# Norm factors moved behind the products, raw rows of x transposed beside the last sum, three chunks in the first feed-forward

## What is computed

```python
def rms_norm(x, g):
    y = x * rsqrt(mean(x * x, axis=-1) + EPS)
    return y * g
# first block, for each of 2 layers
h = rms_norm(x, attn_norm[l]); proj = h @ w_in[l]       # q k v, u, latent (c_q, c_kv, k_rope)
x = x + mixed @ w_out[l]
h = rms_norm(x, ffn_norm[l])
x = x + (silu(h @ w_gate[l]) * (h @ w_up[l])) @ w_down[l]
# second block, for each of 2 layers
h = rmsnorm(x, norm_mix); q_a, k_a, v_a, f_a, q_b, kv_b, g_b, gate_a, gate_b = split(h @ w_in)
log_f = log_sigmoid(f_a + b_forget)
y_a = fox_attention(q_a, k_a, v_a, log_f) @ w_o_fox
y_b = nsa(q_b, kv_b, g_b) @ w_o_nsa
x = x + (sigmoid(gate_a) * y_a + sigmoid(gate_b) * y_b) @ w_out
h = rmsnorm(x, norm_mlp); x = x + square(relu(h @ w_up)) @ w_down
# at the end: rmsnorm(x, norm_final)
```

## Time and profile before

| | |
|---|---|
| median of 3 runs | 3001.28 us (3000.63 to 3008.34) |
| the profiled execution | 3002.22 us, its span 3000.2 us |
| PE busy | 2834.8 us (94%) |
| DVE busy | 1394.8 us (46%) |
| ACT busy | 1090.4 us (36%) |
| granted TensorE clock, mean | 0.963 of full |

### The profile page before, as it was taken

How to read it: one execution, slowest core, us unless ns; L and a number is a source line. 1 busy time by engine, 2 the same in 40 slices (tenths; PEclk the granted TensorE clock), 3 DMA queues, 4 the chain that set the end, 5 groups by cost and what they waited for, 6 DMA issues and landing times.

```text
span 3000.2 us, 34972 instructions
## 1 busy us (share of the span) xinstructions
PE 2834.8 (94%) x14016; PEld 2348.5 (78%) x14016; DVE 1394.8 (46%) x2486; ACT 1090.4 (36%) x1941; POOL 14.5 (0%) x29
## 2 busy tenths in 40 slices
PE   5889999998899999999799999999999899999998
PEld 5677888887678888788688878888787788778886
DVE  6764333347643333456464344242556554353343
ACT  3453222234542223344353233142454442242231
POOL 1000000000000000000000000000000000000000
PEclk8889999999899999999799999999999899999999
DMA  4102332321023332222102323323213013323231
GB/s 123 52 8 78 98 99 86 106 75 59 1 71 98 99 98 96 70 77 71 57 1 84 106 77 99 95 88 100 72 47 116 8 36 92 98 91 101 90 105 56
DMA packets 186147, 231.41 MB, mean 77 GB/s; under 512 B 11794, under 2 KB 140148, under 8 KB 185988
## 3 DMA queue, kind: packets, MB, share of 16 engines
q1 hardware_dynamic: 184436, 225.95, 24.3%
q0 software_dynamic: 976, 1.32, 0.3%
q10 hardware_dynamic: 576, 1.92, 0.2%
HBM read 227.05 MB, written 2.11 MB: 76 GB/s over the span
## 4 chain that ended last, share of the span: by engine, by line
PE 87%; DVE 9%; ACT 2%; issue 2%; SPq 0%; DMA 0%; DVEq 0%; ACTq 0%
PE bank L504 25%; PE bank L506 24%; PE bank L505 24%; PE bank L638 4%; PE bank L623 2%; PE bank L694 1%; PE bank L693 1%; PE bank L597 1%; PE bank L867 1%; DVE Wl L1760 1%; DVE RS L1852 1%; PE bank L704 1%; PE bank L689 0%; DVE TMP L1909 0%; ACT TMP L1232 0%
## 5 line engine op out<-in xcount | busy, mean ns | idle before, releaser
L1760 DVE TENSOR_TENSOR Wl<-RAW,Wh 128x1024 fp32r<-128x1024 f32 (+1 forms) x430 | 508.6, 1209 | 699.4 <-ACT Wh L1176 699.1
L504 PE MATMUL bank<-Hh,Wh 128*128 128x512 f32 (+1 forms) x1680 | 660.5, 393 | 0.1
L506 PE MATMUL bank<-Hh,Wl 128*128 128x512 f32 (+1 forms) x1680 | 656.0, 390 | 0.0
L505 PE MATMUL bank<-Hl,Wh 128*128 128x512 f32 (+1 forms) x1680 | 655.7, 390 | 0.0
L1176 ACT ACTIVATE Wh<-RAW 128x1024 fp32r<-128x1024 f32 (+1 forms) x430 | 436.3, 1044 | 488.6 <-PE bank L506 488.3
L506 PEld LDWEIGHTS bank<-Hh,Wl 128*128 128x128 f32 (+1 forms) x1680 | 315.0, 188 | 68.3 <-issue 0.5
L504 PEld LDWEIGHTS bank<-Hh,Wh 128*128 128x128 f32 (+1 forms) x1680 | 315.8, 188 | 66.5 <-issue 0.8
L505 PEld LDWEIGHTS bank<-Hl,Wh 128*128 128x128 f32 (+1 forms) x1680 | 315.5, 188 | 66.0 <-issue 0.5
L506 PE MATMUL bank<-Wh,A 128*128 128x512 f32 x864 | 341.7, 396 | 0.0
L505 PE MATMUL bank<-Wl,A 128*128 128x512 f32 x864 | 341.7, 395 | 0.0
L504 PE MATMUL bank<-Wh,A 128*128 128x512 f32 x864 | 341.7, 395 | 0.0
(11 more groups left out here) (349 smaller groups left out, 3435.3 us busy)
## 6 DMA issues: line engine op xcount, KB each, us to landing
RAW<-in_w_up_dram SPq DMA_DIRECT2D x108, 512.0 KB, 4.0
RAW<-in_w_down_dram SPq DMA_DIRECT2D x108, 512.0 KB, 3.9
RAW<-in_w_in_dram SPq DMA_DIRECT2D x90, 512.0 KB, 3.8
RAW<-in_w_gate_dram SPq DMA_DIRECT2D x44, 512.0 KB, 4.1
RAW<-in_w_out_dram SPq DMA_DIRECT2D x32, 512.0 KB, 3.9
RAW<-in_cmp_w_dram SPq DMA_DIRECT2D x16, 512.0 KB, 3.8
RAW<-in_w_o_fox_dram SPq DMA_DIRECT2D x8, 512.0 KB, 3.4
RAW<-in_w_o_nsa_dram SPq DMA_DIRECT2D x8, 512.0 KB, 3.4
```

Of the source, the lines that this page charges most:

```text
L504: pe.matmul(o, sh, mh, start=first, stop=False)
L505: pe.matmul(o, sh, ml, start=False, stop=False)
L506: return pe.matmul(o, sl, mh, start=False, stop=last)
L1760: ve.tensor_tensor(M.Wl[:, v % NHL, 0:n], M.RAW[:, v % NRAW, 0:n], M.Wh[:, v % NHL, 0:n].bitcast(F32), ALU.subtract).then_inc(G.w_lo, 1)
```

## The change

It has four parts.

1. The rows of x are transposed as they are, without a factor. `turn_side(n, 0)` transposes channel tiles 0 to 3 as a side of the second half sum (the first half of the channels is summed by then), and `turn_side(n, 1)` channel tiles 4 to 7 as a side of the next linear's first units. Gains are applied where they were, at the split.
2. The factors are made once per norm for all four row tiles (`factor(n, ...)`, a side of the next linear) and are multiplied onto the results. Where the result has tokens on the partitions it is a per-partition scale in the evacuation (`keep`), and for the feed-forward it goes into the add to x (`add_x`, r, or its square for the squared relu). Where the result has tokens along the columns, the norms of `BY_TOKEN` need the factors as a row on all partitions: PE transposes the broadcast factors (`rb`, four transposes behind the last turn), DVE copies them to SBUF (`RBA`, `RBB`) and multiplies each tile by them (`by_token`) on its way out of PSUM.
3. The first block's feed-forward has its 22 tiles in chunks of 8, 8 and 6 instead of 12 and 10, which frees room for a second pair of split activations, `HA`. The weight units and matmuls are as many as before.
4. In the second block `fg` comes after `fq` instead of ahead of it, and the forget side runs in `fk`. The tiles of `fq` and `fk` are multiplied by DVE into a buffer `OS`; ACT casts from there and DVE subtracts from there. `kc` goes the same way.

```diff
-CHUNKS1 = (12, 10)
+CHUNKS1 = (8, 8, 6)
...
-        plan.append([(f, 0, KD, 8, 32), (g, 8, KD, 24, 32)])
         for c in range(4):
             rows(w, IN2_Q + c * 256, 256, KD, 4)
+            if c == 1:
+                plan.append([(f, 0, KD, 8, 32), (g, 8, KD, 24, 32)])
...
+def sums_before(n):
+    block, l, place = n // 4, n % 4 // 2, n % 2
+    if place:
+        return [f"out{block}{l} {half}" for half in range(2)]
+    block, l = (block, l - 1) if l else (block - 1, DEPTH - 1)
+    return [f"down{block}{l} {len((CHUNKS1, CHUNKS2)[block]) - 1} {half}" for half in range(2)]
...
+BY_TOKEN = (0, 1, 2, 3, 4, 6)
...
+    def turn_side(n, half):
+        for _ in range(1 if half else 4):
+            yield
+        for k in range(4 * half, 4 * half + 4):
+            b = fresh(f"turn{n} {k}")
+            for s in range(NT):
+                if k == 4 * half:
+                    if n:
+                        pe.wait_ge(*K.drained(f"{sums_before(n)[half]} {s}"))
+                    else:
+                        pe.wait_ge(G.x_in[s], 16)
+                i = pe.transpose(b[:, s * P:(s + 1) * P], M.X[:, s, k * P:(k + 1) * P], ident)
+            i.then_inc(*K.fills(f"turn{n} {k}"))
+            yield
+            K.close(f"turn{n} {k}")
+    def factor_side(n):
+        for _ in range(5):
+            yield
+        if n in BY_TOKEN:
+            b = fresh(f"rb{n}")
+            pe.wait_ge(G.rstd, n + 1)
+            for s in range(NT):
+                i = pe.transpose(b[:, s * P:(s + 1) * P], M.r(n, s).to_broadcast([P, P]), ident)
+            i.then_inc(*K.fills(f"rb{n}"))
+    def summed_twice(n, stage):
+        stage(0)
+        if n < N_NORMS:
+            side = begin(turn_side(n, 0))
+        stage(1)
+        if n < N_NORMS:
+            drain(side)
+            turning[n] = begin(turn_side(n, 1))
+            factors[n] = begin(factor_side(n))
...
+    def factor(n, cols):
+        c = cols.stop - cols.start
+        v, y, g = M.RS[:, 1, 0:c], M.RS[:, 0, 0:c], M.RS[:, 2, 0:c]
+        sq = M.SS[:, 16:24].rearrange("p (s h) -> p s h", h=2)[:, cols, :]
+        ve.wait_ge(G.sq, 8 * n + 4 + cols.stop if cols.start or c < NT else 8 * n + 8)
+        ve.scalar_tensor_tensor(v, sq[:, :, 0], EPS, sq[:, :, 1], ALU.add, ALU.add).then_inc(*own.up())
+        rsqrt(c)
         ve.wait_ge(*own.now())
+        ve.tensor_copy(M.r(n)[:, cols], y).then_inc(G.rstd, 1)
+    def by_token(dst, name, n, gain=None):
+        rows = dst.shape[0]
+        b = M.bank[K.of(name)][0:rows, :]
+        ve.wait_ge(*K.full(name))
+        ve.wait_ge(*K.drained(f"rb{n}"))
+        if gain is None:
+            ve.tensor_tensor(dst, b, M.rb(n)[0:rows, :], ALU.mult).then_inc(*K.empties(name))
         def fox_k(c):
             def evac(j, name):
-                packed_k([(M.KAh[:, 4 * c + 2 * j + x, :], M.KAl[:, 4 * c + 2 * j + x, :], None) for x in range(2)], name)
+                ve.wait_ge(G.fox_lo, fox_lo.n - 1)
+                by_token(M.OS[:, j, :], name, n)
+                ve.wait_ge(*hi.due())
+                for x in range(2):
+                    h = 4 * c + 2 * j + x
+                    for r in (0, 64):
+                        i = ve.tensor_tensor(M.KAl[r:r + 64, h, :], M.OS[64 * x:64 * x + 64, j, :], M.KAh[r:r + 64, h, :].bitcast(F32), ALU.subtract)
+                i.then_inc(*fox_lo.up())
...
-        norm(norm_of(1, l, 0), G_NM + 8 * l)
+        n = norm_of(1, l, 0)
...
-        next_unit()
...
-        forget = begin(forget_side())
...
         for c in range(2):
-            lin_t(f"fq{l} {c}", KD, fox_q(c))
+            lin_t(f"fq{l} {c}", KD, fox_q(c), normed(n) if c == 0 else None)
+        next_unit()
+        by_token(M.FGT[0:32, :], f"fg{l}", n)
+        forget = begin(forget_side())
         for c in range(2):
             lin_t(f"fk{l} {c}", KD, fox_k(c))
```

More of the change, by code:

```diff
@@ L575, in at_each, with normed @@
     def at_each(name):
-        ready = set()
+        return once(lambda k: pe.wait_ge(*K.drained(f"{name} {k}")))
+    def normed(n):
         def before(k):
[L580 to L601, removed]
+            if k == 4:
+                drain(turning[n])
+            pe.wait_ge(*K.drained(f"turn{n} {k}"))
+        return once(before)
@@ L921, in forget_side @@
                 yield
+        for c in range(2):
+            lin_t(f"fq{l} {c}", KD, M.Hh, M.Hl, normed(n) if c == 0 else None)
+        b = fresh(f"fg{l}")
+        u, h, lo, _ = next_unit()
+        for k in range(KD):
+            i = three(b[0:32, :], h[:, k, :], lo[:, k, :], M.Hh[:, k, :], M.Hl[:, k, :], k == 0, k == KD - 1)
+        i.then_inc(*K.fills(f"fg{l}"))
+        K.points["unit", u] = K.full(f"fg{l}")
+        K.close(f"fg{l}")
         forget = begin(forget_side())
-        for c in range(2):
-            lin_t(f"fq{l} {c}", KD, M.Hh, M.Hl)
         for c in range(2):
@@ L1183, in lin_t_units @@
             for j in range(2):
-                for k in range(1, ku - 1, 2):
-                    tick()
+                for k in range(ku):
+                    if before:
+                        before(k0 + k)
+                    if k < ku - 1 and k % 2:
+                        tick()
                 if k0 + ku == kt:
@@ L1452, in ffn @@
         n = norm_of(block, l, 1)
-        norm(n, (G_NP if block else G_FN) + 8 * l)
+        before = normed(n)
         if n + 1 == N_NORMS:
@@ new lines, in evac, with turn_side @@
+            if n == N_NORMS and half and s % 2:
+                factor(n, slice(s - 1, s + 1))
+                ve.wait_ge(G.gf_in, 16)
+                for r in (s - 1, s):
+                    ve.scalar_tensor_tensor(M.X[:, r, :], M.X[:, r, :], M.r(n, r), M.GF[:, :], ALU.mult, ALU.mult).then_inc(G.fin, 1)
+        return evac
+    def turn_side(n, half):
+        for _ in range(1 if half else 4):
+            yield
+        for k in range(4 * half, 4 * half + 4):
+            yield
+            name = f"turn{n} {k}"
+            col = gain_column(n) + k
+            lower(M.h(n)[1][:, k, :], M.bank[K.of(name)][:, :], M.h(n)[0][:, k, :], M.GT[:, col:col + 1]).then_inc(*K.empties(name))
@@ L1883, in rope, with normed, before, summed_twice @@
+    def normed(n):
+        def before(k):
+            if k == 4:
+                drain(turning[n])
+        return before
+    def summed_twice(n, stage):
+        stage(0)
+        if n < N_NORMS:
+            side = begin(turn_side(n, 0))
+        stage(1)
+        if n < N_NORMS:
+            drain(side)
+            turning[n] = begin(turn_side(n, 1))
+            factors[n] = begin(factor_side(n))
+    turning, factors = {}, {}
     def rope(x1, x2, c, s, tm):
```

367 lines of the change are left out of this document (199 added, 168 removed).

## The result

| | before | changed |
|---|---|---|
| median | 3004.45 us (4 runs, 3000.63 to 3008.34) | 3021.85 us (4 runs, 3021.0 to 3023.95) |
| profiled execution | 3002.22 us, span 3000.2 | 3022.18 us, span 3020.1 |

The ratio is 1.0059, 95% interval 1.0041 to 1.0076: slower, and beyond the range of 2988 to 3015. The two profiled executions are 19.96 us apart, where the sum had +0.8. The executions of the kernel before fall in two groups, 3000 to 3004 and 3006 to 3009 us (the runs beside the experiments show a mean granted clock of 0.962 to 0.965 in the one and of 0.957 to 0.960 in the other); the profiled one is of the first, so the medians are only 17.4 us apart.

A forecast was written before the change was run, and what follows sets the result against it. TensorE, busy 2834.8 of 3000.2 us, was taken as the bound, so only its waits and lower clock count. Boundaries -21.0, start +1.3, keys +20.2, final norm +0.3 gave +0.8: median 3002 us, range 2988 to 3015.

The forecast's parts named there:

- the sum: Whole kernel: all gains and losses together +0.8 us, median 3002 us; chance 0.50, own range 2993 to 3010.
- The rest: Final norm 0.3 us later; feed-forward and gate multiplications and the third chunk hidden under products; `kc` and gates 0.
- the forecast of no change: Whole kernel: measured time within about 0.3% (9 us) of the kernel before; chance 0.50.
- the two slower rivals: Lower clock after every new wait, 3014 us (chance 0.16); 7.05 us for each key tile, 3010 us (0.09).
- The boundaries: Norms n = 1 to 7: shorter TensorE losses between the sum and the next linear, 21.0 us won together.
- The keys: Fox keys and values: VectorE backlog makes TensorE wait 6.1 and 4.0 us per layer, 20.2 us lost in two layers.
- The slower tile of the rival (7.05): Fox keys: 7.05 us per key tile, each behind one more weight cast, +8.4 us, 3010 us; chance 0.09.
- its faster ones: Fox keys: 4.1 us or less per tile, no backlog, 2982 us (chance 0.11); 4.7 us, half, 2991 us (0.13).
- The start: Up to the latent side: first product some 5.3 us sooner, but VectorE gets 6.4 us more; 1.3 us lost.
- The clock: Rival: every new TensorE wait at boundaries and keys costs 2.2 us of lower clock, +12.2 us, 3014 us; chance 0.16.
- Transposes: Added transposes on TensorE: 0.107 us each, 2.6 us for 24; the skill's 275 ns, not taken, would give 6.6 us.

The follow-up runs named there:

- e14: The changed kernel with `HA` alone moved by 224 bytes, so that it starts equal to the weights modulo 256; 3007.7 us, ratio 1.0003 to the kernel before.
- e4: The changed kernel with the factors made behind the last channel tile's low part and their transposes moved to the second unit's end; 2996.7 us, ratio 0.9972.
- e12: The changed kernel with `HA` alone moved by 32 bytes, which put it 64 off the weights; 3009.0 us, ratio 1.0021 to the kernel before.
- e10: The kernel before with the arena moved to start like `Hh` and `Hl` (128 modulo 256) and the weights 64 bytes further (192); 3031.8 us, one run.
- e5: The kernel before with weights and arena both starting at 160 modulo 256, `Hh` and `Hl` still at 128; 3019.6 us, ratio 1.0044.

## Why the prediction was wrong

**The step that failed** is the one under "The rest": "The third chunk adds eight adds of 0.69 per layer, also under products; its unit and product counts are the same." The counts are the same, the pace isn't. I priced every product at the 0.227 us of the earlier trace rows, a product on `Hh`, and didn't look at one on a tile of the arena, which stood in the same trace at 0.233. What the change adds there isn't work but a place: `HA` starts 32 bytes off the weights modulo 256, and 88 units at 0.16 us make 14.1 us. e14, which alters that one number, takes it back, and comes to the time of before (ratio 1.0003, interval 0.9994 to 1.0012); without this term the forecast of no change, with its range, would have held. The trace had it: 5.60 us for a unit on `A` against 5.44 on `Hh`. No rival named it, so no chance stood for it; the two slower rivals (0.25 together) rest on the clock and on the key tile, and neither is what cost the time.

**The boundaries** were right in kind, and 20.8 us were won of 21.0, with waits of 3.92 for 4.3 at `rb`, 1.55 for 1.85 at n = 2 and 2.35 for 3.0 at n = 5 and 7. That the sum is so close is in part luck: n = 1, 2 and 3 came as forecast, but n = 4 and 6 won 3.3 and 2.3 for 2.5 and 1.3, and n = 5 and 7 only 2.1 and 3.2 for 2.9 and 4.4, in part because the lower clock behind the wait cost 1.6 us (n = 5) and not 0.5. Why n = 4 and 6 won more was not followed up. VectorE was somewhat faster in the factors (280.26 to 282.62 and a copy) than the 2.65 us laid out. e4 shows that the wait came from the place of the factors in VectorE's queue and not from its load.

**The keys** were right: 21.1 us lost for 20.2, 6.1 us for a tile for 6.0 (the casts from `OS` are the 0.1: over the eight key tiles 1.2 us, where the prediction weighed 1.4 and took none). Of the two waits the first was exact and the second 1.2 and 2.5 for 4.0, because the lower clock behind the first took up the rest; the sum of both is the backlog of VectorE, as the text said. The slower tile of the rival (7.05) and its faster ones didn't show.

**The start** lost 2.0 us for 1.3. **The clock** rival is not what happened as a whole: the mean granted clock is 0.963 over 3000.2 us before and 0.964 over 3020.1 us now, some 110 us of full pace lost in either, so the clock is no part of the difference as a whole.

**Transposes.** The rule of the Trainium skill weighed in the prediction ("TensorE: Matmul & The Clock Gate", Part 4, some 275 ns each) would have made a group of four 1.1 us; the page measured bf16, these are fp32. The products on either side of the groups at 274.32 and 276.15 show 0.43 to 0.44 us for a group, as the earlier trace rows does; the row decides. On starts, the Trainium skill's "SBUF — State Buffer", section "Operand start alignment", says that an fp32 operand may start at any multiple of 4 bytes, and that its measurements timed nothing. All tiles here keep to it, so all the places are allowed; the table above shows what they cost in pace.

## What to carry to other kernels

When a change moves an operand, read the pace of the products on the old and on the new place before calling it free; count the matmuls in two equal windows in which TensorE is busy throughout. Lay out the tiles of both operands so that they start equal modulo 256 bytes: here this alone gives 0.8% in the kernel before and 1.3% in the changed one, for a tile of 32 bytes put elsewhere. And a factor that is needed late is made late: behind the parts for which TensorE waits, and no wait for another engine between two steps of a tile when the next tile's step can stand there.

## What the runs showed of the hardware

The pace of fp32r matmuls of 512 columns depended on where the moving and the stationary operand start against each other modulo 256 bytes. At 0 a unit of 24 took 5.44 us (0.2267 each); 32 bytes off, either way and in either role, 5.60 (0.2333); with the moving operand 128 off 5.575; 64 further than the stationary one 5.49 (e12, and in e10 `down` and the units with H stationary), 64 less 5.60 (`Hh` moving in e10). Two groups don't fit: in e10 the units on `MX`, whose operands lie as those on `A`, took 5.60, and in e5 those on `OA` and `ON`, which start where the weights do, 5.46. Why the pace depends on it was not tested; smaller products, other types and starts that differ by other amounts weren't either.
